# A two-layer streaming-encoder trunk: the SBUF tensors allocated in another order, with a filler

## The reference

```
x = layer_norm(x)
for l in range(2):
    sh1, sc1, g1, sh2, sc2, g2 = split(silu(c) @ w_ada[l] + b_ada[l])
    z = (x * (1 + sc1) + sh1) @ w_in[l]
    # four groups: gated MLP, latent attention, diagonal SSM, gated linear recurrence
    ym = rms_norm_per_group(concat(y_a, y_b, y_c, y_d))
    x = layer_norm(ALPHA * x + (1 + g1) * (ym @ w_out[l]))
    h = x * (1 + sc2) + sh2
    a = causal_depthwise_conv3(h @ w_up[l])            # 1024 x 5632
    val, gate = split(a)
    x = layer_norm(ALPHA * x + (1 + g2) * ((val * silu(gate)) @ w_down[l]))   # 2816 x 1024
```

## Time and profile before

| | us |
|---|---|
| median of 3 runs | 1424.63 |
| lowest and highest run | 1419.69 and 1429.35 |
| span of the profiled execution, first to last instruction | 1426.1 |

### The profile page before, as it was taken

How to read it: one execution, slowest core, us unless ns; L and a number is a source line. 1 busy time by engine, 2 the same in 40 slices (tenths; PEclk the granted TensorE clock), 3 DMA queues, 4 the chain that set the end, 5 groups by cost and what they waited for, 6 DMA issues and landing times.

```text
span 1426.1 us, 17247 instructions
## 1 busy us (share of the span) xinstructions
PE 1353.1 (95%) x6866; PEld 1007.3 (71%) x6866; DVE 792.5 (56%) x1389; ACT 509.9 (36%) x770; POOL 535.1 (38%) x327
## 2 busy tenths in 40 slices
PE   6999999999999999898899999999999999989987
PEld 3445676776788888676675577677688888868866
DVE  5985778656766776447663556664743333321134
ACT  2523224335333333332224422442453333332223
POOL 0630100565444444334438010055644444434433
PEclk9998999999999999899999999999999999999998
DMA  9356733032555556453226251102133323222321
GB/s 383 148 118 163 172 123 95 16 103 89 192 193 191 189 180 240 161 177 133 89 66 115 68 80 35 45 17 86 48 104 97 96 89 103 89 74 89 98 65 60
DMA packets 64801, 166.79 MB, mean 117 GB/s; under 512 B 14288, under 2 KB 26960, under 8 KB 64208
## 3 DMA queue, kind: packets, MB, share of 16 engines
q1 hardware_dynamic: 64720, 165.68, 38.0%
HBM read 160.04 MB, written 5.62 MB: 116 GB/s over the span
## 4 chain that ended last, share of the span: by engine, by line
PE 80%; DVE 12%; issue 2%; ACT 2%; DMA 2%; POOL 1%; SPq 0%; ACTq 0%; POOLq 0%
PE bank L478 18%; PE bank L480 18%; PE bank L479 17%; PE bank L569 8%; PE bank L563 3%; PE bank L594 2%; PE bank L493 1%; PE bank L498 1%; PE bank L487 1%; PE bank L722 1%; DVE ada L1201 1%; DVE xa L1140 1%; PE bank L759 1%; DVE xa L1146 1%; PE bank L741 1%
## 5 line engine op out<-in xcount | busy, mean ns | idle before, releaser
L2317 POOL TENSOR_TENSOR ring_r<-ring,scr_r 128x1024 fp32r<-128x1024 f32 x146 | 355.1, 2434 | 458.2 <-ACT scr_r L1904 457.7
L478 PE MATMUL bank<-ym_r,scr_r 128*128 128x512 f32 x688 | 274.4, 399 | 4.6 <-DVE hm_r L1756 3.6
L480 PE MATMUL bank<-hm_r,scr_r 128*128 128x512 f32 x688 | 273.6, 398 | 0.0
L479 PE MATMUL bank<-ym_r,ring_r 128*128 128x512 f32 x688 | 271.0, 394 | 0.0
L478 PE MATMUL bank<-scr_r 128*128 128x512 f32 x480 | 197.9, 412 | 35.3 <-DVE scr_r L1802 17.1
L479 PE MATMUL bank<-scr_r,ring_r 128*128 128x512 f32 x480 | 192.0, 400 | 0.0
L1784 DVE SCALAR_TENSOR_TENSOR scr<-bank,pb,scr 128x511 f32<-128x511 f32 x86 | 64.5, 749 | 196.9 <-ACT scr L2167 196.7
L1904 ACT ACTIVATE scr_r<-ring 128x1024 fp32r<-128x1024 f32 x146 | 152.8, 1048 | 39.3 <-DMA ring<-in_w_up 16.7
L569 PE MATMUL bank<-hm,ring 128*128 128x512 f32 x336 | 165.2, 633 | 0.0
L478 PEld LDWEIGHTS bank<-ym_r,scr_r 128*128 128x128 f32 x688 | 129.7, 189 | 36.9 <-issue 5.2
L1201 DVE SCALAR_TENSOR_TENSOR ada<-ada,silu_c 128x1024 f32<-128x1024 f32 x80 | 137.2, 1718 | 32.1 <-DMA ada<-in_w_ada 32.1
(11 more groups left out here) (369 smaller groups left out, 1774.9 us busy)
## 6 DMA issues: line engine op xcount, KB each, us to landing
ring<-in_w_up SPq DMA_DIRECT2D x88, 512.0 KB, 3.7
ada<-in_w_ada SPq DMA_DIRECT2D x80, 512.0 KB, 3.7
ring<-in_w_down SPq DMA_DIRECT2D x44, 512.0 KB, 3.6
ring<-in_w_in SPq DMA_DIRECT2D x33, 512.0 KB, 5.0
scr<-in_w_ada SPq DMA_DIRECT2D x16, 512.0 KB, 14.4
ring<-in_w_out SPq DMA_DIRECT2D x16, 512.0 KB, 3.6
pa<-in_par_a SPq DMA_DIRECT2D x2, 2144.5 KB, 13.0
xa<-in_x SPq DMA_DIRECT2D x1, 2048.0 KB, 8.3
```

Source lines behind the costliest of these rows:

```text
L478: first = mm(dst, w_hi, x_hi, start=start, stop=False)
L479: mm(dst, w_lo, x_hi, start=False, stop=False)
L480: return first, mm(dst, w_hi, x_lo, start=False, stop=stop)
L2317: G.tensor_tensor(ring_r[:, at, :], ring[:, at, :], high[:, at, :].bitcast(F32), ALU.subtract)\
```

## The change

The four lines that allocate `xa`, `hm`, `ym` and `ring` move behind the small tensors, and a tensor `margin` of 424 float32 per partition, which no instruction reads or writes, is put ahead of them.

```
+MARGIN = 424
...
-        xa = sb("xa", [P, KD, T])
-        hm, hm_r = twins("hm", [P, KD, T])
-        ym, ym_r = twins("ym", [P, KD, T])
-        ring, ring_r = twins("ring", [P, RING, SLOT])
         ada = sb("ada", [P, ARING, D])
         silu_c = sb("silu_c", [P, D])
         mods = sb("mods", [P, L * MOD_L])
...
         small = sb("small", [P, 96])
         neg_half = sb("neg_half", [P, 16])
         steps_t = sb("steps_t", [P, NSC])
+        sb("margin", [P, MARGIN])
+        xa = sb("xa", [P, KD, T])
+        hm, hm_r = twins("hm", [P, KD, T])
+        ym, ym_r = twins("ym", [P, KD, T])
+        ring, ring_r = twins("ring", [P, RING, SLOT])
         scr, scr_r = twins("scr", [P, SCRATCH])
```

## The result

The changed kernel takes 1402.91 us (median of 4 runs, 1401.79 to 1405.01); the kernel before, with one more run beside it, 1426.1 us (1419.69 to 1429.35). The ratio is 0.985, with a 95% interval of 0.9816 to 0.9884. The forecast of 1424 us and its range of 1409 to 1437 us missed it. The two medians differ by 23 us, but the kernel before has only four runs here.

What follows compares the result with a forecast made beforehand. The prediction took TensorE, busy 95%, to bound the kernel. All terms were 0, summing to 0 on the profiled 1426.1 us; the forecast was set at the runs' median, 1424 us, range 1409 to 1437 us.

Steps and rivals of the forecast that it cites:

- the part on TensorE: Matmul operand reads: moving operand, weights and their pair; each taken as 0 change from the new start addresses.
- the pair: Weights and moving operand sharing a remainder, as in L479: taken as 0, with ends of -14.6 us and +17.5 us.
- The moving operand and the crossing: Up and down projections: neither the moving operand's remainder nor crossing a 16,384-byte boundary costs anything; taken as 0.
- The weights: The norm's sums: 0.111, 0.111 and 0.107 us each for weights in `xa`, `hm`, `scr`; weight placement taken as 0.
- The first rival: All float32r matmul groups come to L479's times: 14.6 us less, 1410 us; chance 0.09.
- The second rival: Float32r matmuls' extra 20 ns at full clock come from placement and vanish: 70 us less, 1354 us; chance 0.03.
- The third rival: Operands at one remainder collide in each of 3504 matmuls, up to 5 ns each: 17.5 us more, 1442 us; chance 0.08.
- The last doubt: An address dependence that only sets in at remainder 0, of which the trace can't tell; no size given.
- the terms for them: ScalarE copies and DMA landings of large chunks: each taken as 0, with +-2 us kept for other engines and for DMA.
- the 0 for DMA: Transfers on the chain, 2% or 28.5 us of it: taken as 0 change, with ends of 2 us either way.

Runs made afterwards that it cites:

- the first kernel of matmuls: Only float32r matmuls of 128x512 on one tensor, 72 in each of 34 groups with own offsets, other engines idle; 0.2267 us a matmul with all offsets 0.
- the two kernels named beside its rows: Kernel before with the filler ahead of `scr` alone, 1423.32 us; changed kernel without its filler, 1404.23 us.

## Why the prediction was wrong

**The step that failed** is the part on TensorE, and in it the reading of "the pair": "the sum over a triple, 0.700 us both where the moving operand shares L479's remainder and where it doesn't", taken as a sign that placement costs nothing, so that this term stood in the sum at 0. The two triples compared both had a mismatch. The up projection has its high weights at 96 and the rest at 128 past a multiple of 256, the down projection its low weights at 128 and the rest at 96. Lines L67 and L68 of the first kernel of matmuls, which repeat these two cases, have 0.2333 and 0.2332 us, and the same matmuls without a mismatch 0.2267. In the place of the 0 the runs show 6.7 ns for each matmul at full clock, 17.8 us in the stages. Two equal numbers came from one cost that both bore; no row of the trace of before had all operands matched, so there was nothing quick to compare with.

**The moving operand and the crossing.** That a tile may cross a multiple of 16,384 bytes at no cost was right: with all five tensors at 128 past it, each last tile crosses and the pace is short. That the moving operand's own remainder doesn't matter was right too, and it didn't help: what matters is its relation to the others.

**The weights.** The norm's sums are plain float32, and these don't feel a mismatch (0.430 against 0.429 us at 512 columns; eight of the norm's sums took 0.89 us before and after). I took a row of one type as evidence for another.

**The bounds.** The first rival had the right sign and the right object, and was mis-sized: it put L479's mean as the floor for all, 14.6 us. But L479 itself came down, from 394 to 390 ns. At full clock the term is 0.0067 us a matmul, 3504 x 0.0067 = 23 us at most; the stages show 17.8 us. In the two up projections 6.04 + 6.25 = 12.3 us of 2064 x 0.0067 = 13.8 us arrive, in the out and down projections only 5.5 of 9.6. Part of these runs at half clock, and the waits for VectorE at the down projection grew a little (L1804, 18.4 us in all against 17.1); I didn't trace the rest. The second rival's 20 ns of each matmul were for one third placement: 6.7 ns went, 13.3 stayed. Its argument against, that a cause in placement should show some spread, was wrong: a triple of 700 ns came out of quite different mismatches. The third rival was upside down: operands with one remainder are the quick case. The last doubt, a dependence that only sets in at remainder 0, is out too: the changed order without the filler has all five tensors 96 past a multiple of 256, and it is as quick.

**What was right.** No instruction, wait or transfer was added or taken away. ScalarE's copies and the landings of the large chunks kept their times (627 and 632 ns, 3.7 us), and the terms for them are 0. The smaller transfers into `scr` did land sooner, which the prediction didn't look at; that this is worth nothing in the total is shown by the two kernels named beside its rows, and the 0 for DMA holds.

## What to carry to other kernels

Before a chain of float32r matmuls with 512 columns is called bound by its columns, look at the distance between starts: 0.2267 us is the best that was seen here, 0.2333 was seen where weights and moving operands don't share their start's remainder of 256 bytes, and 32 bytes of filler took 1.3% off the whole kernel. Read the pace of a stage in the profile, too, and not only the total: the total of this kernel moves by some us with the stretches of half clock, and the up projection repeats to 0.1 us. When a trace is to show that a property costs nothing, there must be a row without the property; two equal rows that both have it show nothing, and a row of another data type doesn't stand in.

## What the runs showed of the hardware

- Float32r matmuls of 128x128 by 512 columns at full clock take 0.2267 to 0.2274 us from start to start with all starts at one remainder of 256 bytes (remainders 0, 32, 64, 96 and 128 tried), and 0.2286 to 0.234 where, at multiples of 32, they differ by 32 to 224 bytes. It is seen with all other engines idle.
- A mismatch adds 2 to 7 ns at 512 columns (6.7 in the kernel before), 3.3 at 480, 2.5 at 448, 2.4 at 384 and none at 320 and 256 (one mismatch tried for each width but 512).
- At half clock (0.426 us), in plain float32 (0.429) and in bfloat16 (0.2158) no such cost was found.
- With starts off the multiples of 32 bytes the same matmul took from 0.2267 to 0.2400 us.
- A transfer of 128 KB into `scr` (`scr<-s_w`) landed after 6.0 to 6.6 us where `scr` starts at a multiple of 256 bytes and after 7.1 to 8.3 us where it starts 96 or 128 past one; for the 512 KB chunks of `w_up` into `ring` no difference was seen (3.6 or 3.7 us). The total didn't change by it.
